# Two filling pieces behind the first head pair of a level, and one masked copy for two heads

## The reference

```python
def step(state, inp):                       # per chunk, for every head
    qc, kc, vc, gc = inp
    b = jnp.cumsum(gc, axis=2)              # gc = log of the forget gate
    diff = b[:, :, :, None, :] - b[:, :, None, :, :]
    decay = jnp.exp(jnp.minimum(diff, 0.0)) * tri[:, :, None]
    A = jnp.einsum('bhtsd,bhsd->bhts', qc[:, :, :, None, :] * decay, kc)
    o = (jnp.einsum('bhts,bhsv->bhtv', A, vc)
         + jnp.einsum('bhtd,bhdv->bhtv', qc * jnp.exp(b), state))
    ...
# in each layer
h = x @ w_in[l]                             # 1024 x 6048 weights
...
y = jnp.concatenate([y_hg * jax.nn.silu(hg_gate), y_mla * ..., y_mem * ...], axis=-1)
x = _layernorm(DEEPNORM_ALPHA * x + y @ w_out[l], ln_g[l], ln_b[l])
```

## Time and profile before

| | |
|---|---|
| median of the timed runs | 2243.11 us (2241.99 to 2243.89) |
| profiled execution | 2246.55 us |
| its span, first to last instruction | 2244.8 us |
| mean granted TensorE clock | 0.99 |
| PE busy | 2165.8 us (96%) |
| DVE busy | 863.8 us (38%) |
| ACT busy | 790.5 us (35%) |
| POOL busy | 891.7 us (40%) |
| chain that ended last, share of PE | 51% |

### The profile page before, as it was taken

One profiled execution on the slowest core, in us unless ns is written; L12 is line 12 of the kernel. 1 busy time (PEld: TensorE's weight loads), 2 busy tenths in 40 slices (PEclk: granted clock), 3 DMA queues, 4 the chain that ended last, 5 costly groups with the idle time before them and its releaser, 6 DMA issues.

```text
span 2244.8 us, 30234 instructions
## 1 busy us (share of the span) xinstructions
PE 2165.8 (96%) x12268; PEld 1768.3 (79%) x12268; DVE 863.8 (38%) x1653; ACT 790.5 (35%) x1605; POOL 891.7 (40%) x704
## 2 busy tenths in 40 slices
PE   7999999999999999999899999999999999999997
PEld 7878887677888878667788888887778787888876
DVE  3063553524355373444521222353511442222263
ACT  4414225444333324444431222244433332222245
POOL 6633424222442432323254544443335345444432
PEclk9999999999999999999999999999999999999999
DMA  6521212112221212212142323222223214322222
GB/s 218 185 76 57 88 48 94 51 52 77 94 76 57 91 54 67 76 39 75 66 128 78 113 94 98 99 95 85 70 86 112 75 57 141 103 94 94 94 73 78
DMA packets 98811, 196.97 MB, mean 88 GB/s; under 512 B 3697, under 2 KB 12273, under 8 KB 98289
## 3 DMA queue, kind: packets, MB, share of 16 engines
q1 hardware_dynamic: 95072, 183.25, 25.0%
q10 hardware_dynamic: 3600, 11.80, 1.6%
HBM read 192.93 MB, written 2.10 MB: 87 GB/s over the span
## 4 chain that ended last, share of the span: by engine, by line
PE 51%; DVE 6%; ACT 3%; DMA 1%; issue 0%; DVEq 0%; ACTq 0%
PE ps L816 16%; PE ps L817 15%; PE ps L818 15%; DVE work L1783 1%; DVE xs L1775 1%; DVE work L1762 1%; PE ps L917 1%; PE ps L926 1%; PE ps L906 0%; PE ps L1058 0%; ACT work L1361 0%; PE ps L1069 0%; DVE side L1466 0%; PE ps L909 0%; PE ps L1039 0%
## 5 line engine op out<-in xcount | busy, mean ns | idle before, releaser
L765 POOL TENSOR_TENSOR wl<-raw,wh 128x512 fp32r<-128x512 f32 (+2 forms) x700 | 891.5, 1307 | 1321.4 <-ACT wh L1114 1321.4
L1114 ACT CAST wh<-raw 128x512 fp32r<-128x512 f32 (+2 forms) x700 | 371.0, 602 | 835.0 <-PE ps L818 693.8
L816 PE MATMUL ps<-xh,wh 128*128 128x512 f32 (+1 forms) x1376 | 518.1, 376 | 0.8 <-issue 0.8
L818 PE MATMUL ps<-xh,wl 128*128 128x512 f32 (+1 forms) x1376 | 510.3, 371 | 0.0
L817 PE MATMUL ps<-xl,wh 128*128 128x512 f32 (+1 forms) x1376 | 510.1, 371 | 0.0
L816 PEld LDWEIGHTS ps<-xh,wh 128*128 128x128 f32 x1376 | 260.9, 190 | 53.5 <-issue 10.4
L818 PEld LDWEIGHTS ps<-xh,wl 128*128 128x128 f32 x1376 | 260.3, 189 | 44.7
L817 PEld LDWEIGHTS ps<-xl,wh 128*128 128x128 f32 x1376 | 260.7, 189 | 41.9
L816 PE MATMUL ps<-wh,xh 128*128 128x512 f32 (+1 forms) x608 | 241.3, 397 | 2.0 <-issue 2.0
L817 PE MATMUL ps<-wl,xh 128*128 128x512 f32 (+1 forms) x608 | 236.3, 389 | 0.0
L818 PE MATMUL ps<-wh,xl 128*128 128x512 f32 (+1 forms) x608 | 236.2, 388 | 0.0
(11 more groups left out here) (253 smaller groups left out, 2459.6 us busy)
## 6 DMA issues: line engine op xcount, KB each, us to landing
raw<-w_in SPq DMA_DIRECT2D x58, 1024.0 KB, 5.2
raw<-w_out SPq DMA_DIRECT2D x20, 1024.0 KB, 5.1
raw<-f1g SPq DMA_DIRECT2D x10, 1024.0 KB, 5.1
raw<-f1u SPq DMA_DIRECT2D x10, 1024.0 KB, 5.0
raw<-f1d SPq DMA_DIRECT2D x10, 1024.0 KB, 5.1
raw<-f2g SPq DMA_DIRECT2D x10, 1024.0 KB, 5.1
raw<-f2u SPq DMA_DIRECT2D x10, 1024.0 KB, 5.1
raw<-f2d SPq DMA_DIRECT2D x10, 1024.0 KB, 5.0
```

The source lines that it names most:

```text
L765: pool.tensor_tensor(wl[s], raw[:, u % 2, k, 0:b.width], wh[s].bitcast(F32), ALU.subtract).then_inc(low_done, 1)
L816: pe.matmul(o, still[0], move[0], start=k0 + k == 0, stop=False)
L818: mm = pe.matmul(o, still[1], move[0], start=False, stop=k0 + k == b.ktiles - 1)
L1114: act.copy(wh[:, u % 3, k, 0:b.width], raw[:, u % 2, k, 0:b.width]).then_inc(high_done, 1)
```

## The change

Two edits.

First, in `beside` the number of slots of a level over which its pieces are spread is 1 instead of 2. In the first group nothing moves, since a level's single piece is in slot 0 in both. In the second group both pieces of a level go to slot 0, behind the first head pair. Slot 1 is empty there.

Second, in VectorE's levels 2 to 7 the masked copies of a pair's two heads, which were one instruction each (128 elements per partition), are one instruction (256 elements per partition, over two PSUM banks), with the mask repeated by a step of 0. This applies to all four groups.

```diff
@@ beside @@
     for ph, n in shares:
         first = 1 if len(ph.slots) > 1 and ph.kind != "level" else 0
-        room = len(ph.slots) - first
+        room = len(ph.slots) - first if ph.kind != "level" else 1
         for i in range(n):
             ph.slots[first + i * room // n].append(pieces.pop(0))
@@ VectorE, level @@
                             size = 2 ** (e.level - 2)
                             m = level_mask[:, e.level - 2, :].rearrange("p (b i) -> p b i", i=size).unsqueeze(
-                                1).to_broadcast([P, T, 32 // size, size])
-                            for h in (2 * pair, 2 * pair + 1):
-                                ins = dve.copy_predicated(
-                                    A_in[:, h].rearrange("p c (b two i) -> p c b two i", two=2, i=size)[:, :, :, 1, :],
-                                    m, ps[:, 4 + h, 0:128].rearrange("p (c b i) -> p c b i", c=T, i=size))
+                                1).unsqueeze(1).to_broadcast([P, 2, T, 32 // size, size])
+                            ins = dve.copy_predicated(
+                                A_in[:, heads].rearrange("p h c (b two i) -> p h c b two i", two=2, i=size)[
+                                    :, :, :, :, 1, :],
+                                m, ps[:, banks, 0:128].rearrange("p h (c b i) -> p h c b i", c=T, i=size))
                         step_done(ins)
```

## The result

The changed kernel takes 2270.55 us (median of 4 runs, 2267.17 to 2275.05) against 2243.5 (4 runs, 2241.99 to 2245.59) for the kernel before beside it: ratio 1.0116, 95% interval 1.0104 to 1.0128. It is slower by 27 us, or 1.2%. The forecast was 2262.5 us in a range of 2251 to 2271. The direction, the place and the mechanism were right; the loss was larger than the 19.3 us of the sum, and near to that of rival D.

What follows compares the result with a forecast made beforehand. The second head group's levels were taken as bound by TensorE's own issue. Per layer -1.4 + 4.6 + 1.2 + 2.3 = +6.7; two layers +13.4, first groups -0.3, clock +6.2: +19.3, giving 2262.5 us, range 2251 to 2271.

Steps and rivals of the forecast that it cites:

- rival D: Second head groups: TensorE's clock is lowered at nearly every new wait; +24 to +26 us, 2268 to 2270; chance 0.17.
- levels 0 to 3: Second head group, gate pieces read by ScalarE: a level takes 7.66 instead of 8.00 us, gain 1.4 us per layer.
- crossing to 5: Level 4 to 5, second group: TensorE waits 1.8 us for VectorE behind two readings; distance 9.52 instead of 8.0 us.
- crossing to 6: Level 5 to 6, second group: 1.8 us wait plus 2.1 us that VectorE loses to POOL's splitting.
- crossing to 7: Level 6 to 7, second group: TensorE waits 1.8 us behind two readings; distance 9.52 instead of 8.0 us, +1.52.
- level 7 to the transposes: Last product pieces are read ahead of the final pair's block; TensorE waits 2.3 us per layer, bounds 0.2 to 2.6.
- POOL's loss on the urgent block: First pair's block of level 6: L1712 to L1714 take 3.7 against 1.6 us beside POOL's splitting, 2.1 us lost.
- the clock term of the sum: Second groups: TensorE's clock drops at new waits; two losses of 1.55 us per layer, 6.2 in all, bounds 0 to 12.4.
- The merged copy: All four groups: 0.42 us, gain 0.07 each, none for the two lowest masks; -0.3 us in all on the path.
- Rival A: Readings not on the path, saved wide-narrow changes come through; 3.3 us per layer faster, 2236 us; chance 0.04.
- B: POOL's losses miss the urgent block and the clock stays; 2.5 us per layer, +4.7 with first groups, 2248; chance 0.10.
- C: POOL's losses land on the urgent block, TensorE's clock is lowered at most once; +13 to +15 us, 2257; chance 0.24.

Runs made afterwards that it cites:

- spread_reads: The change with VectorE's readings put back behind the second pair's block and the next level's first pair's block, TensorE's order kept: 2241.17 us, ratio 0.9983.
- short_pool: The change with POOL's subtraction cut to 8 columns for two units in each layer, their low parts not computed: 2257.83 us, ratio 1.0065.
- double_read: The change plus one more VectorE sum of the same size behind each level's second product piece, levels 4 to 7: 2272.46 us, ratio 1.0135.
- fill_waits: The change plus useless wide matmuls (7, 16 and 7) on TensorE at the crossings to levels 5, 6 and 7: 2260.7 us, ratio 1.0079.
- spread_7_split: The change with VectorE's readings put back and level 7's pieces one behind each pair again: 2239.36 us, ratio 0.9978 to the kernel before.

## Why the prediction was right, and where its sizes were off

The forecast of the direction rested on one step: VectorE's list follows the slots, so both readings stand in front of the next level's urgent block. That step held in the trace, wait by wait. `spread_reads` moved nothing but these readings and turned a loss of 27 us into a gain of 3.6.

Term by term, per layer, from the starts of the levels' first pieces; the forecast column is without the clock, the measured one has it in it:

| step | forecast | measured |
|---|---|---|
| levels 0 to 3 | 4 x 7.66 = 30.6 us | 31.2 (7.65, 7.66, 8.19, 7.70) |
| crossing to 5, distance | 9.52, wait 1.8 | 9.54, wait 1.69 |
| crossing to 6 | 9.52 + 2.1 = 11.62 | 12.44, wait 3.77 |
| crossing to 7 | 9.52 | 11.63, wait 1.62 |
| level 7 to the transposes | 13.65, wait 2.3 | 14.83, wait 2.68 |
| sum | 74.9 | 79.64 |

The waits are right to 0.4 us. The one at level 3 (0.35) I had named and taken as nothing; it cost 0.5 with the split of a double narrow block. POOL's loss on the urgent block, 2.1 us, was right (2.07 by `short_pool`). The Trainium skill's rule of an exclusive lock ("SBUF — State Buffer", the two separate sides) was taken in the prediction for an estimate of up to three whole POOL instructions, 3.8 us, which this block did not reach: its three operations took 0.52, 0.86 and 0.73 us more than alone. In kind the trace agrees: each of them ends just behind one of POOL's, and in `double_read` a block started 0.6 later ends at nearly the same time. (The rows that the prediction names for the readings and copies lie outside of POOL's run. Inside it, 301.86 to 306.94 before, a reading at 305.89 takes 0.68 us and the two copies at 306.49 take 0.48, so the statement holds.)

The step that was mis-sized is the clock term of the sum. The forecast put 2 x 1.55 = 3.1 us per layer into the sum, counted on the filling pieces alone, and said that part of a slow stretch "can fall on narrow matmuls", meaning that this would be cheap. It is not: a narrow block at the lower clock takes 1.92 or 1.97 instead of 1.12 or 1.15 us. Two such blocks cost 1.6, and the pieces behind them 6.99 and 6.29 us against 5.68 (305.93 to 312.92 and 317.56 to 323.85, against 293.49 to 299.17), 1.9 more. That is 3.5 us in the stage, and 3.4 by `fill_waits`. A further slow stretch starts at the key transposes, which take 2.61 us: from their start to that of the next block (L997) it is 5.24 us instead of 3.58 in layer 0, and 5.23 instead of 3.57 in layer 1, 1.7 more. So 5.2 us per layer and not 3.1, which is 4.1 us too little in all; the wait at level 3 adds 1.1 and the longer wait at the transposes 0.8. Against that the rest of the profiled execution came out 4.5 us shorter (the spans' 21.4, less 22.6 in the stages and 3.3 behind them), so that between the two profiled executions there are 21.6 us, 2.3 more than the sum. I give no cause for the 4.5: the first second group starts anywhere between 251.31 (`spread_reads`) and 255.43 us (`spread_7_split`) in runs whose work ahead of it is the same. That the timed medians differ by 27 stays open: the change's profiled execution lies among its faster runs (2268.18, median 2270.55), that of before above its median (2246.55, 2243.11).

The merged copy was sized right (0.43 for 0.42) and its effect wrong by the 0.3 us that didn't come. Rival A needed the readings off the path, and they were on it; B needed another alignment with POOL, and it was the one forecast (L1712 at 6.86 and POOL's run at 6.46 us behind the first piece, against 6.84 and 6.45). C, the clock lowered at most once, is out as well. D, the clock lowered at nearly every new wait, is what the profiled execution shows: it fell at three of the four waits per layer, and the timed loss of 27 us is a little above D's 24 to 26. The forecast, two losses per layer, was a guess between C and D, and nothing in the rows before could decide it. That the median stands inside the range is luck in part: it is 0.45 us from the upper end, and two of the four runs lie above it.

## What to carry to other kernels

Where an engine reads results late and in the order of a slot list, moving the slots on one engine moves the readings on another: look at what stands in front of the other engine's urgent work, and count the move by latency from its last wait, not by busy share. A reading that waits for the newest result belongs behind the block that someone waits for. Waits between short matmuls can also lower TensorE's clock for the work behind them. In the change's trace it fell after 3.77, 1.62 and 2.68 us and not after the 1.69 of the first crossing; in layer 1 of `short_pool` it fell after that 1.69 as well. So a microsecond of waiting cost about one and a half in that execution (9.8 us of waits at the three crossings and the transposes, 5.2 us of clock), and can cost less or more in another; price it by a range. Such a wait can be filled where it can't be removed.

## What the runs showed of the hardware that I had not expected

- Narrow float32 matmuls (x32, 32 columns) are slowed by the lower clock as the wide ones are: 1.92 us against 1.12, a factor of 1.7.
- The granted clock fell to 0.50 just before 302 us, within the wait that had begun at 300.30, so the drop can come while the engine is still idle and cover the restart.
- The same program with the same waits has the low clock for 3.4 us in one layer and 13.7 in the other (`short_pool`), and the stage takes 72.76 and 77.39 us.
- Thirty wide matmuls of no use per layer made the changed kernel 9.8 us faster, and its timed runs agreed within 0.8 us.
- A VectorE block that starts 0.6 us later inside a POOL run can end only 0.08 later, and a copy made 0.06 us shorter ahead of such a block gains nothing.
